# Two heads' scores on the array's two row halves, values on its two column halves, and the softmax division moved ahead of the transposes

## The reference

```python
s = jnp.einsum('bnqkgd,bnskd->bnkgqs', qb, kb) * (ATT_HEAD_DIM ** -0.5)
s = s - slopes[None, None, :, :, None, None] * dist[None, :, None, None]
s = jnp.where(mask[None, :, None, None], s, -jnp.inf)
mx = jnp.maximum(jnp.max(s, axis=-1), sink)
p = jnp.exp(s - mx[..., None])
den = jnp.sum(p, axis=-1) + jnp.exp(sink - mx)
o = jnp.einsum('bnkgqs,bnskd->bnqkgd', p / den[..., None], vb)
...
x = x + jnp.concatenate([h_m, o_a], axis=-1) @ w_out
x = x + jnp.square(jax.nn.relu(_rmsnorm(x, g_mlp) @ w_up)) @ w_down
x = x + jax.nn.sigmoid(_rmsnorm(x, g_ple) @ w_ple_gate) * (p @ w_ple_proj)
```

## Time and profile before

| | us |
|---|---|
| median of 3 runs | 2938.96 |
| the profiled execution | 2933.94 |
| its span | 2932.1 |
| TensorE busy in the span | 2808.2 (96%) |
| VectorE busy | 1337.8 (46%) |
| ScalarE busy | 745.8 (25%) |

### The profile page before, as it was taken

How to read it: one execution, slowest core, us unless ns; L and a number is a source line. 1 busy time by engine, 2 the same in 40 slices (tenths; PEclk the granted TensorE clock), 3 DMA queues, 4 the chain that set the end, 5 groups by cost and what they waited for, 6 DMA issues and landing times. The chain is left out here.

```text
span 2932.1 us, 37716 instructions
## 1 busy us (share of the span) xinstructions
PE 2808.2 (96%) x14885; PEld 2427.8 (83%) x14885; DVE 1337.8 (46%) x1997; ACT 745.8 (25%) x1408; POOL 75.6 (3%) x163
## 2 busy tenths in 40 slices
PE   7999999789999996999999999799999999997998
PEld 6889888578888875888888888689898999995887
DVE  6566565533333324443443443543534444444443
ACT  4333333332222223121121121311121212113332
POOL 0000000000000001000000000100000000000110
PEclk9999999889999997999999999899999999998999
DMA  5111211332222213111111111511111011114221
GB/s 187 63 63 50 75 51 50 132 119 72 78 75 79 69 34 124 58 43 43 57 43 43 57 43 43 190 51 36 52 34 57 29 57 36 50 50 168 79 81 46
DMA packets 90368, 202.95 MB, mean 69 GB/s; under 512 B 9592, under 2 KB 47576, under 8 KB 90296
## 3 DMA queue, kind: packets, MB, share of 16 engines
q1 hardware_dynamic: 89096, 197.63, 20.2%
q0 software_dynamic: 1200, 4.33, 0.4%
HBM read 153.59 MB, written 48.44 MB: 69 GB/s over the span
## 5 line engine op out<-in xcount | busy, mean ns | idle before, releaser
L98 PE MATMUL f_up<-f_hT_hi,f_up_hi 128*128 128x352 f32 (+1 forms) x1280 | 451.6, 353 | 10.2 <-DVE f_hT_lo L1652 10.1
L100 PE MATMUL f_up<-f_hT_hi,f_up_lo 128*128 128x352 f32 (+1 forms) x1280 | 450.6, 352 | 0.0
L99 PE MATMUL f_up<-f_hT_lo,f_up_hi 128*128 128x352 f32 (+1 forms) x1280 | 450.5, 352 | 0.0
L1674 DVE TENSOR_TENSOR f_acc<-f_acc,f_down 128x1024 f32<-128x1024 f32 (+1 forms) x272 | 331.8, 1220 | 223.1 <-PE f_down L100 221.8
L98 PE MATMUL f_down<-f_down_hi,f_uT_hi 128*128 128x512 f32 x1088 | 425.1, 391 | 0.0
L99 PE MATMUL f_down<-f_down_lo,f_uT_hi 128*128 128x512 f32 x1088 | 424.5, 390 | 0.0
L100 PE MATMUL f_down<-f_down_hi,f_uT_lo 128*128 128x512 f32 x1088 | 424.4, 390 | 0.0
L1685 DVE TENSOR_TENSOR f_u<-f_u 128x704 f32<-128x704 f32 (+1 forms) x80 | 82.1, 1026 | 541.3 <-ACT f_u L1553 541.3
L98 PEld LDWEIGHTS f_up<-f_hT_hi,f_up_hi 128*128 128x128 f32 x1280 | 242.1, 189 | 35.0 <-issue 6.9
L99 PEld LDWEIGHTS f_up<-f_hT_lo,f_up_hi 128*128 128x128 f32 x1280 | 242.0, 189 | 23.5
L100 PEld LDWEIGHTS f_up<-f_hT_hi,f_up_lo 128*128 128x128 f32 x1280 | 242.1, 189 | 22.5
(11 more groups left out here) (335 smaller groups left out, 4585.3 us busy)
## 6 DMA issues: line engine op xcount, KB each, us to landing
f_raw<-in_w_up SPq DMA_DIRECT2D x64, 512.0 KB, 3.6
f_raw<-in_w_down SPq DMA_DIRECT2D x64, 512.0 KB, 3.6
hT_hi_kept<-m_hT_hi SPq DMA_DIRECT2D x17, 512.0 KB, 5.0
hT_lo_kept<-m_hT_lo SPq DMA_DIRECT2D x17, 512.0 KB, 5.8
a_hT_hi<-hT_hi_kept SPq DMA_DIRECT2D x17, 512.0 KB, 3.6
a_hT_lo<-hT_lo_kept SPq DMA_DIRECT2D x17, 512.0 KB, 4.5
m_x<-in_x_prompt SPq DMA_DIRECT2D x16, 512.0 KB, 4.2
a_x_sum<-in_x_prompt SPq DMA_DIRECT2D x16, 512.0 KB, 3.5
```

The lines of the kernel that those rows point to most:

```text
L98: eng.matmul(out, lh(k), rh(k), start=f, stop=False)
L99: eng.matmul(out, lh(k), rl(k), start=False, stop=False)
L100: ins = eng.matmul(out, ll(k), rh(k), start=False, stop=e)
L1674: dve.tensor_tensor(acc[0:t.n, n, :], acc[0:t.n, n, :], down_ps[n % 2][0:t.n, :], ALU.add).then_inc(added, 1)
```

## The change

Four parts, all in `attention_programs`.

1. Scores: q is no longer regrouped, so each transposed block of `qT` holds two heads that share a key/value head, one in each half of the partitions. Keys are stored twice (`k_twice`, `ck_twice`), so that `kT` holds the same key head in both halves. `score(t, g)` alternates between the two halves (b), which write two different PSUM banks. The heads are kept in the order 0, 2, 1, 3 (`HEAD_AT`) inside a group; biases, sinks and the rows of w_out follow it, so pieces 4 to 7 of w_out are loaded as two transfers of 64 rows each.
2. Values: `average(t)` holds the values (128 keys by 64 channels) and streams `sT` of four heads (512 columns). Group g writes partitions g * 64 to g * 64 + 63, that is, it uses one half of the array's columns. Both groups are done in one call, once a round, with the result already channel-major in `outT`, which alternates between two banks by tile.
3. The division: `share` multiplies the exponentials (128x1024) by the reciprocal of the sum before `turn_s`, which now waits for it.
4. The attention result is not transposed any more; `turn_heads` transposes only `heads_in`. `mixT_hi` and `mixT_lo` are made in two parts, from `outT` and from `turned`, and the output projection waits for the second behind `score(mid, 1)` instead of in front of it.

```diff
+    k_twice, ck_twice = sb("k_twice", [P, KVH, 2, HD]), sb("ck_twice", [P, KVH, 2, HD])
-    kT, ckT = sb("kT", [P, 2, P]), sb("ckT", [P, P])
+    kT, ckT = sb("kT", [P, 2, KVH, P]), sb("ckT", [P, KVH, P])
-    out_ps = [m.acc[:, 2 * g:2 * g + 2, :].rearrange("p a b -> p (a b)") for g in (0, 1)]
+    outT = [m.acc[:, 2 * n:2 * n + 2, :].rearrange("p a (b t) -> p (a b) t", t=P) for n in (0, 1)]
-    SOFT, AVG, N_CONST = 5, 3, 3
+    SOFT, SHARE, N_CONST = 5, 3, 3
+    HEAD_AT = [0, 2, 1, 3]
...
-            sp.dma_start(wo_raw[slot][:], w_out[c * P:(c + 1) * P, :]).then_inc(wo_in[slot // 2], 16)
+            if c < HEADS:
+                sp.dma_start(wo_raw[slot][:], w_out[c * P:(c + 1) * P, :]).then_inc(wo_in[slot // 2], 16)
+            else:
+                for g in range(KVH):
+                    row = MW + (g * GRP + HEAD_AT[c - HEADS]) * HD
+                    sp.dma_start(wo_raw[slot][g * HD:(g + 1) * HD, :], w_out[row:row + HD, :]).then_inc(wo_in[slot // 2], 16)
...
         def take_q(t):
             all_of(act, q_ps, t.i)
             all_of(act, qk_turned, t.i - 1)
-            act.activation(q[0:t.n, :].rearrange("p (h g d) -> p g h d", g=KVH, h=GRP),
-                           proj[0][0:t.n, :].rearrange("p (g h d) -> p g h d", g=KVH, h=GRP), ACT.Copy).then_inc(q_sb, 1)
+            act.activation(q[0:t.n, :], proj[0][0:t.n, :], ACT.Copy).then_inc(q_sb, 1)
...
             if exists(old.i):
-                all_of(act, mix_turned, old.i)
+                all_of(act, out_done, old.i)
                 all_of(act, o1_ps, old.i - 1)
                 act.wait_ge(w_lo_made, W_PIECES)
-                act.activation(mixT_hi[:, :, 0:old.n], turned[:, :, 0:old.n], ACT.Copy).then_inc(mix_hi, 1)
+                act.activation(mixT_hi[:, HEADS:KC, 0:old.n], outT[slot][:, :, 0:old.n], ACT.Copy).then_inc(mix_hi, 1)
+                all_of(act, mix_turned, old.i)
+                act.activation(mixT_hi[:, 0:HEADS, 0:old.n], turned[:, 0:HEADS, 0:old.n], ACT.Copy).then_inc(mix_hi, 1)
...
-        def turn(t, src, done):
-            for c in range(KC):
-                ins = pe.transpose(turned[:, c, 0:t.n], src(c), ident[0:t.n, 0:t.n])
-            ins.then_inc(done, 1)
+        def turn_heads(t):
+            slot_loaded(pe, heads_loaded, t)
+            for c in range(HEADS):
+                ins = pe.transpose(turned[:, c, 0:t.n], heads_in[0:t.n, t.slot, c * P:(c + 1) * P], ident[0:t.n, 0:t.n])
+            ins.then_inc(mix_turned, 1)
...
-                pe.wait_ge(consts_in, 16 * N_CONST)
-                pe.transpose(turned[:, GRP + 1, :], ck[:], ident[:])
-            pe.transpose(turned[:, GRP, 0:t.n], kv[0:t.n, t.slot, 0:KVW], ident[0:t.n, 0:t.n]).then_inc(qk_turned, 1)
+                for g in range(KVH):
+                    pe.transpose(turned[:, GRP + KVH + g, :], ck_twice[:, g].rearrange("p b d -> p (b d)"), ident[:])
+            for g in range(KVH):
+                ins = pe.transpose(turned[:, GRP + g, 0:t.n], k_twice[0:t.n, g].rearrange("p b d -> p (b d)"), ident[0:t.n, 0:t.n])
+            ins.then_inc(qk_turned, 1)
...
         def score(t, g):
-            head = slice(g * HD, (g + 1) * HD)
             reached(pe, soft, (t.i * 2 + g - 1) * SOFT + 1)
-            for h in range(GRP):
+            for a in range(2):
                 for p in parts(t):
                     n = keys(t, p)
-                    kk = kT[head, t.slot, 0:n] if p == CUR else ckT[head, :] if t.n < P else kT[head, 1 - t.slot, :]
-                    ins = pe.matmul(scores[0:t.n, h, p * P:p * P + n], qT[head, h, 0:t.n], kk, start=True, stop=True)
+                    for b in range(2):
+                        rows = slice(b * HD, (b + 1) * HD)
+                        kk = kT[rows, t.slot, g, 0:n] if p == CUR else ckT[rows, g, :] if t.n < P else kT[rows, 1 - t.slot, g, :]
+                        ins = pe.matmul(scores[0:t.n, 2 * b + a, p * P:p * P + n], qT[rows, 2 * g + a, 0:t.n], kk, start=True, stop=True)
             ins.then_inc(scores_ps, 1)
...
-            reached(pe, exps, (t.i * 2 + g) * 2 + 1)
+            reached(pe, shared, (t.i * 2 + g + 1) * SHARE)
...
-        def average(t, g):
-            reached(pe, sT_sb, t.i * 2 + g + 1)
-            reached(pe, averaged, ((t.i - 1) * 2 + g + 1) * AVG)
-            for h in range(GRP):
-                for p in parts(t):
-                    n = keys(t, p)
+        def average(t):
+            all_of(pe, sT_sb, t.i, 2)
+            all_of(pe, mix_lo, t.i - 2, 2)
+            for p in parts(t):
+                n = keys(t, p)
+                for g in range(KVH):
                     vals = kv[0:n, t.slot, KVW + g * HD:KVW + (g + 1) * HD] if p == CUR else (cv if t.n < P else v_prev)[:, g * HD:(g + 1) * HD]
-                    ins = pe.matmul(out_ps[g][0:t.n, h * HD:(h + 1) * HD], sT[0:n, g, p, h, 0:t.n], vals,
+                    ins = pe.matmul(outT[t.slot][g * HD:(g + 1) * HD, :, 0:t.n], vals, sT[0:n, g, p, :, 0:t.n],
                                     start=p == parts(t)[0], stop=p == CUR)
             ins.then_inc(out_done, 1)
...
             if exists(old.i):
-                average(old, 1)
+                if exists(r - 1):
+                    reached(pe, v_kept, r - 2)
+                if on_round(r, 2):
+                    pe.wait_ge(*m.heads_done)
+                average(old)
+                turn_heads(old)
             if exists(cur.i):
                 project_q(cur, second).then_inc(q_ps, 1)
-            if exists(old.i):
-                reached(pe, averaged, (old.i + 1) * 2 * AVG)
-                slot_loaded(pe, heads_loaded, old)
-                turn(old, lambda c: (heads_in if c < HEADS else att)[0:old.n, old.slot, c % HEADS * P:(c % HEADS + 1) * P], mix_turned)
...
-            if exists(old.i):
-                all_of(pe, mix_lo, old.i)
             if exists(mid.i):
             if exists(old.i):
                 all_of(pe, q_sb, r if exists(r) else NT)
+                all_of(pe, mix_lo, old.i, 2)
                 project_out(0, first)
             if exists(mid.i):
                 turn_s(mid, 0)
             if exists(old.i):
                 project_out(0, second).then_inc(o0_ps, 1)
-            if exists(mid.i):
-                if exists(cur.i):
-                    reached(pe, v_kept, r - 1)
-                if on_round(r, 1):
-                    pe.wait_ge(*m.heads_done)
-                average(mid, 0)
-            if exists(old.i):
                 all_of(pe, kv_sb, r if exists(r) else NT)
                 project_out(1, first)
             if exists(cur.i):
...
-        def split(i, hi_made, lo, hi, n, lo_made):
-            all_of(dve, hi_made, i)
-            dve.tensor_tensor(lo, turned[:, :, 0:n], hi, ALU.subtract).then_inc(lo_made, 1)
+        def split_mix(t):
+            n = t.n
+            reached(dve, mix_hi, t.i * 2 + 1)
+            dve.tensor_tensor(mixT_lo[:, HEADS:KC, 0:n], outT[t.slot][:, :, 0:n], mixT_hi[:, HEADS:KC, 0:n], ALU.subtract).then_inc(mix_lo, 1)
+            reached(dve, mix_hi, t.i * 2 + 2)
+            dve.tensor_tensor(mixT_lo[:, 0:HEADS, 0:n], turned[:, 0:HEADS, 0:n], mixT_hi[:, 0:HEADS, 0:n], ALU.subtract).then_inc(mix_lo, 1)
...
-        def divide(t, g):
-            n, base = t.n, (t.i * 2 + g) * AVG
+        def share(t, g):
+            n, base, (lo, hi) = t.n, (t.i * 2 + g) * SHARE, key_span(t)
             f = lambda a: mx[0:n, g, a, :]
             reached(dve, exps, (t.i * 2 + g + 1) * 2)
-            dve.tensor_tensor(f(DEN), f(SUM), f(SINK_EXP), ALU.add).then_inc(averaged, 1)
-            dve.wait_ge(averaged, base + 1)
-            dve.reciprocal(f(DEN), f(DEN)).then_inc(averaged, 1)
-            dve.wait_ge(averaged, base + 2)
-            reached(dve, out_done, t.i * 2 + g + 1)
-            all_of(dve, mix_turned, t.i - 2)
-            dst = att[0:n, t.slot, g * GRP * HD:(g + 1) * GRP * HD].rearrange("p (h d) -> p h d", h=GRP)
-            dve.tensor_tensor(dst, out_ps[g][0:n, 0:GRP * HD].rearrange("p (h d) -> p h d", h=GRP),
-                              f(DEN).unsqueeze(2).to_broadcast([n, GRP, HD]), ALU.mult).then_inc(averaged, 1)
+            dve.tensor_tensor(f(DEN), f(SUM), f(SINK_EXP), ALU.add).then_inc(shared, 1)
+            dve.wait_ge(shared, base + 1)
+            dve.reciprocal(f(DEN), f(DEN)).then_inc(shared, 1)
+            dve.wait_ge(shared, base + 2)
+            part = s[0:n, g, :, lo:hi]
+            dve.tensor_tensor(part, part, f(DEN).unsqueeze(2).to_broadcast([n, GRP, hi - lo]), ALU.mult).then_inc(shared, 1)
...
         def take_kv(t):
             all_of(dve, kv_ps, t.i)
+            all_of(dve, qk_turned, t.i - 1)
+            keys_in = proj[1][0:t.n, 0:KVW].rearrange("p (g d) -> p g d", g=KVH)
+            dve.tensor_copy(k_twice[0:t.n], keys_in.unsqueeze(2).to_broadcast([t.n, KVH, 2, HD]))
             dve.tensor_copy(kv[0:t.n, t.slot, :], proj[1][0:t.n, 0:KV]).then_inc(kv_sb, 1)
...
```

(24 more changed lines are left out.)

6 lines of the change are left out of this document (2 added, 4 removed).

## The result

The changed kernel took 2871.39 us (median of four runs, 2869.61 to 2874.65) beside 2938.61 for the kernel before (2936.87 to 2940.35): a ratio of 0.9775, interval 0.9762 to 0.9787. It is faster, by 67 us. The profiled execution took 2874.65 us, its span is 2872.8.

A forecast was written before the change was run, and what follows sets the result against it. TensorE's work was taken to bound the attention rounds (busy 468.06 of 470.00 us). Gains of 26.7, 16.2, 4.8 and 7 less 1.3 make 53.4; 2933.9 less 53.4 plus 5.0 gives 2885.5, said as 2886, range 2873 to 2900.

The forecast's parts named there:

- Scores: Score blocks: alternating row halves overlap in order, 9 slots of 0.12, 1.08 us instead of 1.97; 26.7 us over 30 blocks.
- Values: Value block: 5 in-order slots of 0.45 plus 0.25 for shape changes, 2.50 us; gain 1.08 a tile, 16.2 us.
- perfect pairs: Score and value blocks: passes of the two halves pair completely, giving 10 us more than the sum.
- Transposes: Attention rounds: four transposes of the attention result go, one for keys is added; 0.32 a tile, 4.8 us gained.
- Tail: Last rounds: scores ahead of the mixT_lo wait, no division before the transposes, shorter last chain; 7 us gained, ends 0 and 9.
- Start: Stage start: doubled w_out issues cost 0.9 and the uncovered multiply in round 1 0.4; 1.3 us lost, ends 0 and 4.
- Multiply: VectorE's 128x1024 multiply before the transposes: priced 1.23 us, finished 1.0 us before TensorE wants it, so hidden.
- From the profile to the median: Whole kernel: 5.0 us added to the sum because the profiled execution took 2933.94 against a median of 2938.96.
- loads as the limit: Score blocks: moving data overlap but loads do not, 16 loads of 0.11, 1.76 us a block; 2906 us, chance 0.13.
- column halves that do not run together: Value blocks: no overlap between column halves, 3.85 us a block, 20 us lost against the sum; 2906 us, chance 0.12.
- nothing overlapping: Score and value blocks: no two passes run at once, only transposes and tail gain; 2933 us, chance 0.15.
- each change of half drains the array: Score and value blocks: every change of half costs 0.11 us with no overlap; 2961 us, chance 0.12.

The follow-up runs named there:

- values by group: Changed kernel with both value matmuls of key/value group 0 issued first, then both of group 1: 2873.46 us, ratio 0.9778.
- scores half by half: Changed kernel with the four score matmuls of one row half issued first, then the four of the other: 2889.27 us, ratio 0.9837.
- runs of two: Changed kernel with the row half changing after every two score matmuls (four passes) instead of after every one: 2876.30 us, ratio 0.9786.

## Why the prediction was right in kind and low in size

- **Scores**: the number is right by luck. 1.08 predicted, 1.09 measured, 0.88 x 30 = 26.4. The working was nine slots of 0.12 in order. The records show eight full pairs 0.11 apart and 0.2 us for entry and exit, which the prediction had left out: two errors that cancel.
- **Values**: the step that failed. "5 slots" came from passes starting in order, with one slot lost at each end, and from 0.45 a pass. The runs show four full pairs of 0.43, and the order does not matter: a matmul of the other half starts ahead of one that waits. 2.50 was predicted, 1.95 measured: 0.55 a tile, 8.3 us over 15. Most of it is the slot (0.45), the rest the pass and the change of shape. I named perfect pairs as worth 10 more and put them at the edge of the range instead of weighing them as a case.
- **Transposes**: right, as far as the round's sum shows it: 3.73 less 3.39 for scores and values leaves 0.34, 0.32 predicted.
- **Tail**: 7.0 in my terms with 1.1 counted in the rounds. The wait moved behind the scores and the last chain is 1.95 (2.2 said), as worked out. What the sum leaves for it is 3.4 higher. Of this 1.6 is the clock of the last projection, 0.77 before and 1.00 after, which I had not priced and which is luck, since the changed kernel run again has 0.77. Another 0.8 lies in the steady stretch: its first score block runs at the lower level in both profiles, 3.71 us before and 2.01 after, and so gains 1.70 instead of 0.88. The remaining 1.0 is spread over the pieces of the tail.
- **Start**: 1.3 predicted, 2.9 measured: 2.3 up to the first softmax step, where 0.9 was said for the doubled issues, and 0.6 behind it, where 0.4 was said. The bound of 4 held. That the loads of w_out are on this path is shown by loading them early. That the 2.3 is the second issue is not shown: the edit that took it away also cut the number of DMA engines, and the transfers of 64 rows may be slower by themselves. While the late pieces were loaded and converted, DMA moved 234 GB/s at a share of 0.90 (585.30 to 597.80), and 288 at 0.81 before the change (579.90 to 592.00).
- **Multiply**: right, 1.3 of cover; with 2.5 us more in front of it the round grows as the cover says.
- **From the profile to the median**: 5.0 us were added, because the profile of before lay that far under its median. That of the change lies 3.3 above. The difference is between executions and does not carry over. This is the second term that failed: taken as fixed, it lifted the forecast by 5.0.

In one line: 8.3 for the values and 3.4 in the tail, less 0.3 in the scores and 1.6 at the start, make 63.2 instead of 53.4 (8.3 + 3.4 - 0.3 - 1.6 = 9.8). From 2933.9 that gives 2870.7. The changed kernel's profile reads 2874.65 by its later start of 3.4, and its median is 2871.39; the 5.0 is the other part of the miss. The same stretches of the changed kernel run again add up to a gain of 62.9. The medians lie 67.2 apart; where the other 4 us are, no profile shows.

Of the rivals, loads as the limit (a score block of 1.76), column halves that do not run together (a value block of 3.6) and nothing overlapping (a score block of 2.0) are excluded by the blocks of 1.09 and 1.87. That each change of half drains the array would make a score block of 2.7 and is excluded by 1.09, and by the orders: in the scores the one that changes half most often, after every two passes, is the cheapest of three.

The Trainium skill, "TensorEngine Tiling (Array Packing)", Key Properties, says that tiles in different places of the array load and multiply in parallel; the trace agrees, 1.97 to 1.09 for row halves and 3.58 to 1.87 for column halves. The Trainium skill, "TensorE: Matmul & The Clock Gate", Part 3, has matmuls start strictly in order of the queue. The row halves in blocks of eight passes (1.64 instead of 1.97, the second half's first pass beside the first half's fifth) and the values by group (1.88, recorded out of the program's order) speak against that across halves.

The three changed orders agree in one thing: a source matmul started while one of the other half was still waiting ahead of it, and in the scores half by half it did not start while two or three were. That also goes with the 0.10 that runs of two cost in the scores and not in the values: there each half has only one run in a block, so no later run starts without its load.

Open: whether one waiting matmul is the limit in other shapes, since no run here tried any. That a transfer of two groups runs on two engines is read from its busy share and the page; a version with 64 as its slowest dimension was not tried.

## What to carry to other kernels

Two F32 matmuls that need only half of the array's rows or columns, put on different halves and writing different banks, cost as much as one here (score blocks of 128 columns, value blocks of 512). In the scores, changing the half after every matmul was best, after every two nearly as good (1.19 against 1.09 us), after every four clearly worse (1.64). When a mechanism comes with a "perfect" case, ask what would prevent it and give it its own chance. When a priced number comes out right, compare the single records with the working behind it before calling it right. Compare a small stretch between the same two operations of each profile: it agrees to about 1 us where whole executions differ by 5. Check the slowest dimension of a transfer before merging two into one.

## What the runs showed of the hardware that was not expected

- A matmul of the other half starts ahead of a queued one: with eight passes in a row the second half begins beside the fifth pass of the first (0.55 us), and the block takes 1.64 us; with four in a row it takes 1.19, in turn 1.09.
- The second F32 pass of a score block starts 0.21 us after the first, the others follow at 0.11, and a run whose weight load starts only with it (runs of two, third run) has the 0.21 again.
- An F32 pass of 512 columns costs 0.43 us with 64 stationary columns, and two on the two column halves cost no more than one.
- A transfer whose source is two groups of 64 rows ran at 50 GB/s, DMA share 0.13, against 195 GB/s at 0.67 in the change's load.
- The granted clock of the last projection, over the same 26 records, was 1.00 in one execution of the changed kernel and 0.77 in another (5.83 and 7.42 us), with TensorE busy 19.02 of 23.01 and 18.98 of 22.98 us ahead of it.
